# Local-attention units of the latent rows set behind the feature steps of four projection tiles, and one Silu for four gates

## The reference

```python
h = _rms_norm(x, g_mix_pre[l])
proj = h @ w_in[l]
aq, ak, av, dqkv, dgate, dalpha, dbeta = jnp.split(proj, IN_SPLITS_2, axis=-1)
aq = _rope(...); ak = _rope(...)
attn_o = _window_attention(aq, ak, av, attn_sink[l])   # block of 128 rows sees itself and its neighbours
dn_o = _gated_deltanet(dqkv, dgate, dalpha, dbeta, ...)
# _window_attention: 8 query heads, 2 key heads, head width 64
#   scores -> mask -> m = max(row max, sink) -> exp -> denom = sum + exp(sink - m) -> p / denom @ v
# _gated_deltanet: conv over rows, silu, q and k scaled to unit length, scan in both directions,
#   o * rsqrt(mean(o * o)) * g_out * silu(gate)
```

## Time and profile before

| | us |
|---|---|
| median of 3 runs | 1665.62 |
| lowest, highest | 1665.32, 1668.08 |
| the profiled execution's own time | 1668.08 |
| its span in the trace | 1666.3 |
| PE busy in the span | 1608.3 (97%) |
| ACT busy | 705.7 (42%) |
| DVE busy | 876.4 (53%) |

### The profile page before, as it was taken

How to read it: one execution, slowest core, us unless ns; L and a number is a source line. 1 busy time by engine, 2 the same in 40 slices (tenths; PEclk the granted TensorE clock), 3 DMA queues, 4 the chain that set the end, 5 groups by cost and what they waited for, 6 DMA issues and landing times.

```text
span 1666.3 us, 28387 instructions
## 1 busy us (share of the span) xinstructions
PE 1608.3 (97%) x11626; PEld 1318.5 (79%) x11626; DVE 876.4 (53%) x1626; ACT 705.7 (42%) x1098; POOL 560.0 (34%) x315
## 2 busy tenths in 40 slices
PE   6999999999999999999999999999999999999997
PEld 3888888878878877778677769887787788888886
DVE  3678756454340276555767488764453744444003
ACT  5435132364354525363536886244344422222232
POOL 1001122293222412463134302524345244444442
PEclk9999999999999999999999999999999999999999
DMA  9574111310222222402322202202202233233332
GB/s 372 191 251 152 52 53 40 128 39 27 64 101 64 77 65 65 143 11 89 132 83 84 87 14 66 63 23 79 94 22 89 78 100 101 89 101 101 102 106 71
DMA packets 43995, 152.69 MB, mean 92 GB/s; under 512 B 4576, under 2 KB 7904, under 8 KB 43616
## 3 DMA queue, kind: packets, MB, share of 16 engines
q1 hardware_dynamic: 40320, 141.81, 25.9%
q10 hardware_dynamic: 3552, 9.13, 1.5%
HBM read 146.72 MB, written 4.19 MB: 91 GB/s over the span
## 4 chain that ended last, share of the span: by engine, by line
PE 86%; DVE 5%; ACT 4%; issue 2%; DMA 2%; SPq 0%; POOL 0%; DVEq 0%; ACTq 0%
PE wide_ps L2075 57%; PE wide_ps L2132 2%; DMA ring<-weights 2%; PE wide_ps L2154 2%; PE pair_ps L2437 1%; PE duo_ps L2466 1%; PE wide_ps L2423 1%; PE wide_ps L2181 1%; PE wide_ps L2700 1%; PE wide_ps L2159 1%; PE duo_ps L2883 1%; PE wide_ps L2581 1%; PE wide_ps L2604 1%; PE pair_ps L2581 1%; PE wide_ps L2864 1%
## 5 line engine op out<-in xcount | busy, mean ns | idle before, releaser
L643 POOL TENSOR_TENSOR ring_r<-ring,scratch_r 128x1024 fp32r<-128x1024 f32 x150 | 369.0, 2461 | 796.3 <-ACT scratch_r L828 769.2
L2075 PE MATMUL wide_ps<-xn_r,scratch_r 128*128 128x512 f32 x1240 | 454.8, 367 | 0.0
L2075 PE MATMUL wide_ps<-work_r,scratch_r 128*128 128x512 f32 (+1 forms) x1081 | 411.7, 381 | 1.8 <-POOL ring_r L643 1.5
L2075 PE MATMUL wide_ps<-work_r,ring_r 128*128 128x512 f32 (+1 forms) x1081 | 397.2, 367 | 0.0
L828 ACT ACTIVATE scratch_r<-ring 128x1024 fp32r<-128x1024 f32 x169 | 178.6, 1058 | 419.7 <-PE wide_ps L2075 401.5
L2075 PEld LDWEIGHTS wide_ps<-xn_r,scratch_r 128*128 128x128 f32 x1240 | 233.4, 188 | 42.2 <-issue 5.1
L2075 PEld LDWEIGHTS wide_ps<-work_r,scratch_r 128*128 128x128 f32 x1081 | 203.4, 188 | 42.8 <-issue 6.7
L2075 PEld LDWEIGHTS wide_ps<-work_r,ring_r 128*128 128x128 f32 x1081 | 203.0, 188 | 35.1
L2075 PE MATMUL wide_ps<-proj_r,scratch_r 128*128 128x512 f32 x620 | 207.3, 379 | 0.0
L812 ACT ACTIVATE proj<-wide_ps 128x512 f32<-128x512 f32 (+1 forms) x78 | 53.7, 688 | 219.7 <-PE wide_ps L2075 210.6
L2075 PEld LDWEIGHTS wide_ps<-proj_r,scratch_r 128*128 128x128 f32 x620 | 116.5, 188 | 21.8
(11 more groups left out here) (504 smaller groups left out, 2882.9 us busy)
## 6 DMA issues: line engine op xcount, KB each, us to landing
ring<-weights SPq DMA_DIRECT2D x222, 512.0 KB, 3.5
proj<-weights SPq DMA_DIRECT2D x34, 512.0 KB, 4.4
h<-tokens SPq DMA_DIRECT2D x4, 768.0 KB, 10.5
h<-tokens ACTq DMA_DIRECT2D x1, 3072.0 KB, 10.0
out<-h ACTq DMA_DIRECT2D x1, 2048.0 KB, 7.3
h<-out ACTq DMA_DIRECT2D x1, 2048.0 KB, 8.6
out<-h SPq DMA_DIRECT2D x16, 128.0 KB, 1.8
proj<-c_rows SPq DMA_DIRECT2D x1, 1024.0 KB, 7.6
```

The lines of the kernel that those rows point to most:

```text
L643: pool.tensor_tensor(as_r(wt), wt, as_r(w_lead(m)).bitcast(F32), ALU.subtract).then_inc(w_split, 1)
L2075: last = pe.matmul(bank[:, a:b], wt[:, cols], as_r(x[:, a:b]), start=n == 0 and p == 0, stop=n == len(k_order) - 1 and p == 2)
```

## The change

The 19 steps of the attention pipeline become `window_step(n)`. The first 13 stand behind feature steps of the gate tiles 18 to 21. Those have 32 feature steps, numbered 0 to 31 as slots, and step n of the attention stands behind slot 6 + 2n. The last six stand after tile 21. The scores have now one pair of banks (the second halves of `wide_ps`), so the scores of unit n wait for the maximum of unit n - 1. The transposed probabilities take `duo_ps`, the output and the inverses `pair_ps`. The values are transposed ahead of tile 8. The gates are copied out as they are, and one Silu over all four (128x2048) stands in ACT's list behind the copies of the cross attention's keys.

```diff
+        win_bank = lambda r: wide_ps[:, r, 512:1024]
+        WIN_FIRST = 6
+        WIN_BEHIND = (4 * KT - WIN_FIRST) // 2
...
@@ scalar
             for t in range(22):
...
+                if t == DQ2 + 2:
+                    act.wait_ge(v2_ps, 1)
+                    act.activation(v_win, duo_ps[:, 0:LAT].rearrange("p (c f) -> p c f", c=NLAT), ACT.Copy).then_inc(v2_ready, 1)
+                if t >= DG2:
+                    break
                 leads_after("proj_2", t)
-                evacuate("proj_2", t, PLAN["proj_2"] + t + 1, LAT, tile_2[:, t, :], ACT.Copy if t < DG2 else other(ACT.Silu))
+                evacuate("proj_2", t, PLAN["proj_2"] + t + 1, LAT, tile_2[:, t, :])
...
+            for q in (10, 11):
+                convolved(q)
+            length_root(7)
...
             for n in range(len(WIN) + 2):
+                if n % 4 == 0 and n < len(WIN):
+                    t = DG2 + n // 4
+                    leads_after("proj_2", t)
+                    evacuate("proj_2", t, PLAN["proj_2"] + t + 1, LAT, tile_2[:, t, :])
                 if n >= 2:
                     window_transposed(n - 2)
...
+            gates_2 = tile_2[:, DG2:DG2 + 4, :]
+            act.activation(gates_2, gates_2, other(ACT.Silu))
+            logs_and_exps()
@@ vector
-            query_key_length(7)
             for n in range(len(WIN) + 4):
...
+                if n == 1:
+                    query_key_length(7)
@@ tensor
+            def window_step(n):
+                if n < len(WIN):
+                    if n:
+                        pe.wait_ge(w_max, n)
...
+                if 2 <= n <= len(WIN) + 1:
+                    m = n - 2
+                    pe.wait_ge(w_exp, 3 * m + 2)
+                    if m:
+                        pe.wait_ge(w_pt, m)
...
+            def window_behind(slot):
+                if slot >= WIN_FIRST and (slot - WIN_FIRST) % 2 == 0:
+                    window_step((slot - WIN_FIRST) // 2)
...
+                    project_split("proj_2", t, range(KT), lead_tile, normed_2, LAT,
+                                  behind=(lambda k: window_behind(KT * (t - DG2) + k)) if t >= DG2 else None)
+            for n in range(WIN_BEHIND, len(WIN) + 3):
+                window_step(n)
```

More of the change, by code:

```diff
@@ L2047, in project, with project_split @@
                         last.then_inc(chunk_used, 1)
-            def project_split(stage, tile, k_order, lead, rest, w, input_ready=None, between=None):
+            def project_split(stage, tile, k_order, lead, rest, w, input_ready=None, between=None, behind=None):
                 g = EVAC[stage] + tile
@@ L2606, in memory_values @@
                 last.then_inc(chunk_used, 1)
+            def window_step(n):
+                if n == 0:
+                    pe.wait_ge(rp_ready, 5)
+                if n < len(WIN):
+                    i, c = WIN[n]
+                    a, b, _, _ = window_keys(c)
+                    if n:
+                        pe.wait_ge(w_max, n)
+                    for r in range(2):
+                        rows = slice(64 * r, 64 * r + 64)
+                        last = pe.matmul(win_bank(r)[:, 0:b - a], tile_2[rows, i, c * CH:(c + 1) * CH], tile_2[rows, AK2, a:b],
+                                         start=True, stop=True)
+                    last.then_inc(w_s, 1)
+                if 2 <= n <= len(WIN) + 1:
+                    m = n - 2
+                    a, b, _, _ = window_keys(WIN[m][1])
+                    pe.wait_ge(w_exp, 3 * m + 2)
+                    if m:
+                        pe.wait_ge(w_pt, m)
+                    else:
+                        pe.wait_ge(v2_ready, 1)
+                    for r in range(2):
+                        for t in range((b - a) // P):
+                            at = r * (b - a) + t * P
+                            last = pe.transpose(win_turned[:, r, t * P:(t + 1) * P], win_probs(m)[:, at:at + P], cst["ident"])
+                    last.then_inc(w_pt_ps, 1)
+                if n >= 3:
+                    m = n - 3
+                    i, c = WIN[m]
+                    a, b, _, _ = window_keys(c)
+                    pe.wait_ge(w_pt, m + 1)
+                    if m >= 2:
+                        pe.wait_ge(w_out_s, m - 1)
+                    else:
+                        pe.wait_ge(l2_rt, 7 + m)
+                    pe.wait_ge(w_p, m + 1)
+                    rows_reciprocal(m, win_inverse)
+                    for t in range((b - a) // P):
+                        for r in range(2):
+                            last = pe.matmul(win_out(m)[64 * r:64 * r + 64], v_win[:, a // P + t, 64 * r:64 * r + 64],
+                                             win_probs_t(m)[:, r * (b - a) // P + t, :],
+                                             start=t == 0, stop=t == (b - a) // P - 1, skip_group_check=True)
+                    last.then_inc(w_o_ps, 1)
@@ L2647, in _ @@
                               stop=True).then_inc(l2_ss, 1)
+                if t == DQ2 + 2:
+                    pe.wait_ge(evacuated, EVAC["proj_2"] + AV2 + 1)
+                    pe.wait_ge(gate_step, G_CUM)
+                    for c in range(NLAT):
+                        last = pe.transpose(duo_ps[:, c * CH:(c + 1) * CH], tile_2[:, AV2, c * CH:(c + 1) * CH], cst["ident"])
+                    last.then_inc(v2_ps, 1)
                 if t == 1:
```

101 lines of the change are left out of this document (32 added, 69 removed).

## The result

| | before | changed |
|---|---|---|
| median, us | 1666.73 (6 runs) | 1673.33 (6 runs) |
| lowest, highest | 1665.16, 1668.08 | 1672.34, 1673.65 |
| the profiled execution's own time | 1668.08 | 1672.88 |
| its span | 1666.3 | 1671.1 |

The ratio is 1.0038, 95% interval 1.0028 to 1.0048: slower, by 4.7 to 8.0 us. The forecast was 1669.8 with a range up to 1672.2. The direction was right, the size too small.

A forecast was written before the change was run, and what follows sets the result against it. PE's own work was taken to set the attention's pace, DVE and ACT following closely. Transposes 0.43 + turns 2.5 + waits 5.1 - gaps 3.8 = +4.2 us on the median 1665.62 gave 1669.8, range 1665.6 to 1672.2.

The forecast's parts named there:

- the two gaps of 3.8 us: PE idle 1.54 us between tile 21 and first scores, plus 2.27 waiting while the attention pipeline fills; the change removes both.
- The rule that a gap in PE costs only its own length: PE's granted clock is 9 tenths or more in all slices, so idle PE time adds nothing beyond itself.
- The values' transposes moved: Four fp32 transposes of 128 columns move ahead of tile 8, where PE has no gap: 0.43 us added.
- Turns: PE switching between part-array attention and whole-array feature matmuls: 0.21 in steps 3 to 12, 0.13 in 0 to 2; 2.5 us.
- The rival that turns are cheap: Turns cost little or hide in PE's waits: +1.7 with nothing for them, 1667.3, up to 1668.9; chance 0.28.
- the waits, 5.1: New PE waits for ACT or DVE at scores 1 to 3, 15, first transposes, ends of tiles 19, 21: 5.1 us.
- Scores 3: PE waits 0.8 us for DVE's maximum of unit 2, which stands behind the inverse of sum 0 and length 7.
- End of tile 19: PE's transposes wait 0.8 us for ACT's lead of tile 21, copy of tile 19 and copy of transposes 2.
- Scores 15: With one pair of banks and no feature steps between, scores 15 wait 0.3 us for the maximum of unit 14.
- Scores 1 and 2: With one pair of banks, PE waits for DVE's maximum of the previous unit: 1.2 us and 0.4 us.
- The Silu: One 128x2048 Silu plus two table loads, 4.5 us, fits ACT's 5.87 us idle, covered by 1.4; uncovered up to 4.5, chance 0.05.
- the base, "a sum of differences holds for both, so on the median: 1665.62 + 4.2": The +4.2 us was added to the median 1665.62, giving 1669.8, and to the profiled execution's 1668.08, giving 1672.3.

The follow-up runs named there:

- the best kernels: Changed kernel with only three or four steps behind feature steps, second pair of score banks from unit 4 or 5: stage -1.93 and -2.23 against before, ratios 0.9988 and 0.9989.
- the one with 64-column matmuls: Kernel with three steps behind feature steps, plus two 64-column matmuls per unit between inverses and value product: stage 165.95, +1.07 against before, ratio 1.0008.

## Why the prediction was right in direction and short in size

- **What bounds the stage.** Right. PE sets the pace, and hiding can give only the two gaps of 3.8 us. That the best kernels gave -1.9 and -2.2, and not more, agrees with it. The rule that a gap in PE costs only its own length was read from clock rows of 9 tenths. It held in the changed kernel and failed in the one with no step behind.
- **The values' transposes moved:** 0.43 forecast, 0.44 in the chain at 871.92.
- **Turns:** right in mechanism, 2.5 forecast. Six feature matmuls between two steps take 1.59, against 6 x 0.227 = 1.36. I had summed 0.21 from pieces and counted 0.13 for steps 0 to 2. Measured are 12 groups at 0.22, one of three matmuls at 0.21 (0.89 to 992.09 against 0.68), and 0.09 at the first scores: 2.9. The rival that turns are cheap is out, and the turn by itself is shown at 0.18. The Trainium skill's rule in "TensorEngine Tiling (Array Packing)", section "Key Properties", that a change of mode drains the engine, has a price of this case beside it. The runs show the price and not the drain.
- **The step of the sum that failed: the waits, 5.1.** They measured 6.0, less the 0.19 that unit 14 waits less than before, 5.8. Each of the seven places was right, and one of 0.15 was missing, at the end of tile 20, where I had written that nothing waits. So it is 6.0 that stands against 5.1. Five of the seven were too small, and three of these make up nearly all of it:
  - Scores 3: 1.26 against 0.8. Of it 0.56 is DVE's operation held by POOL's split. I took 0.2 for that operation from a place where POOL is idle (the earlier trace rows have POOL at 0.00). The change brings POOL's splits into the same time as the attention's small DVE operations, and I asked of POOL only if its result came in time.
  - End of tile 19: 1.15 against 0.8, end of tile 21: 0.84 against 0.6. I added the durations of ACT's three operations and left out the hand-overs: PE's last matmul of slot 15 ends at 959.41 and ACT starts at 959.50, ACT's copy ends at 961.88 and PE starts at 962.03.
  - Scores 15: 0.47 against 0.3, the "some hand-over" I named and took too low. The kernels with one pair show the same 0.18 + 0.40 every four units.
  - Scores 1 and 2 were 0.4 too large in sum. For scores 1 my own rows give 942.94 + 1.33 = 944.27 and not 944.35, and I had left the turn of 0.2 out of PE's time there, which I counted as a turn as well; with both put right it is 0.9, as measured.
- **The gaps taken away:** 3.8, as forecast. 0.44 + 2.9 + 6.0 - 3.8 = 5.5, against 5.40 measured. The remaining 0.1 I don't resolve.
- **The Silu:** cover of 1.4 forecast, 1.36 measured, and shown alone to cost nothing.
- **The other step that failed: the base, "a sum of differences holds for both, so on the median: 1665.62 + 4.2".** It weighs more than the waits. The kernel before's six executions fall into two groups, three of 1665.16 to 1665.62 and three of 1667.84 to 1668.08. The median of three that I built on, 1665.62, is of the lower group. The changed kernel's six lie together, 1672.34 to 1673.65, and all but the lowest have the mean granted clock of 0.996 that the profiled 1668.08 has too. The upper group's mean, 1667.95, and the stage's 5.40 make 1673.35, and 1673.33 was measured. So of the 3.5 us that the forecast of 1669.8 was short, 2.3 are the base and 1.2 the stage. The stage's error alone would have stayed in the range: 1665.62 + 5.40 = 1671.0, under 1672.2. The profiled execution, for which I had 1672.3, took 1672.88: 1.2 more in the stage, 0.56 less ahead of it. That the changed kernel's six held none of the lower group is taken as chance. The kernel that differs from it only in ACT's later tile copies has three such executions, 1668.08 to 1669.68, beside six of 1670.88 to 1671.91. Over the 21 executions of the kernel before that ran beside the last experiments the median is 1667.51.
- **The range.** Its upper bound of 4.3 for the turns comes out at 4.4 by its own terms, (0.30 + 0.20 - 0.12) x 10 + 0.20 x 3, and the "0.5 more of waits" is not in its sum 4.2 + 1.8 = 6.0. Neither decides anything here.

The pieces of the change, by the experiments: hiding the filling is a gain of about 2 us, which three steps behind feature steps have with two pairs of banks. The single pair gives it all back. Seven steps behind are +0.4. From there to the 13 of the change are 5.0 us more: six more turns (1.3), and 3.6 of waits, for the early start brings ACT's conv, root and lead ahead of the first exponentials and DVE's held operation ahead of the maximum of unit 2, and ACT's order adds the waits at tile ends.

## What to carry to other kernels

Where PE is busy up to a pipeline's edges, put only as many steps behind other PE work as it takes to fill the pipeline, here three or four: each further one costs a turn of the array (0.22 us a step here) and lays its ACT and DVE work among lists that are full already. When work moves in time, ask of each engine whose work it moves beside, POOL too, not only whether its result is there: a duration read where POOL idles is not the one beside its split. Set the sum on a base of many runs, and look whether their times fall into groups. On a path that is waited for, add the hand-overs (0.09 us from PE to ACT and 0.15 from ACT to PE here).

## What the runs showed of the hardware

**A DVE operation held by POOL** is not new in this trace, only unseen by me. The kernel before has it at tile 8, DVE and POOL:

```profile
868.71 2.25 DVE L1742 TENSOR_SCALAR state<-proj,par_sb 128x512 f32<-128x512 f32 x1 [3.00 <-ACT proj L812]
```

```profile
868.27 2.40 POOL L643 TENSOR_TENSOR ring_r<-ring,scratch_r 128x1024 fp32r<-128x1024 f32 x1 [3.92 <-ACT scratch_r L828]
```

Its like takes 0.49. It ends 0.29 behind POOL's split, so a part of it must have been done ahead of the release. DVE has slack there, so it cost nothing.

Two more in the kernel before: 2.46 us from 874.18 on, 0.29 behind the split that runs from 873.74 for 2.61, and 0.69 from 881.63 on, 0.27 behind the split from 879.18 for 2.87.

**PE's granted clock** fell to 1.2 GHz in the kernel without steps behind and one pair of banks. In the row 958:962, ahead of the fall, PE is busy 1.40 there. In the kernel before it stayed at 2.4 GHz, with this row for the same stretch:

```profile
958.00:962.00 4.00, 2.18 (x16) 1.21 (x15) 1.53 (x7) 2.66 (x4) 0.00 (x0) 1.00 0.45 131
```

The longest single idle stretch of PE ahead of the fall is the 1.52 us to 960.01. That the idle time brought the clock down is argued from these rows. No run was made to test it.

**A spread of 2 to 3 us between executions** of one kernel comes from the first 70 us, where weights arrive. The windows of 20 to 40 us, of the kernel before and of the one with 64-column matmuls:

```profile
20.00:40.00 20.00, 16.64 (x100) 9.25 (x100) 7.97 (x16) 12.04 (x18) 4.71 (x2) 0.83 1.01 405
```

```profile
20.00:40.00 20.00, 17.07 (x118) 9.56 (x119) 10.32 (x21) 14.00 (x22) 4.71 (x2) 1.00 1.03 413
```

With the clock granted in full there, the first long row of 240 feature matmuls starts at 65.33 and not at 67.89. The code of that stretch is the same. All 13 traces go this way: with 1.00 in this window the long row starts at 64.75 to 65.34 (3 traces), with 0.91 at 66.36 and 66.86, with 0.83 at 67.20 to 68.41 (8 traces). Executions of one kernel split in the same way: of 25 of the kernel before, the 17 with a mean granted clock of 0.996 took 1666.61 to 1668.19, the 7 with 0.998 took 1664.66 to 1665.38. Whether the clock makes the start longer, or weights that arrive later leave PE idle and so lower the clock, no run tells. It is why the stage's length tells more here than the whole time.
